# Moving twelve transposes of expert tiles between two stages, and a switch of row buffers by five rows

## The reference

```python
x += g1 * Mix(RMSNorm(x) * (1 + sc1) + sh1)    # three mixers, merged by gates, then ONE output projection
x += g2 * PEER(RMSNorm(x) * (1 + sc2) + sh2)

def run(xb):                                   # PEER, per block of tokens
    q = (xb @ w_q).reshape(blk, 8, 2, 128)
    s = einsum("thpd,pnd->thpn", q, keys)      # key scores, 2 x 128 sub-keys per head
    sv, si = top_k(s, 16)
    cand = sv[:, :, 0, :, None] + sv[:, :, 1, None, :]
    best, pos = top_k(cand.reshape(blk, 8, 256), 16)     # -> eidx, one of 16384 experts
    g = softmax(best)
    act = gelu(einsum("thkd,td->thk", u_tab[eidx], xb))
    return einsum("thk,thkd->td", g * act, v_tab[eidx])
```

## Time and profile before

| | us |
|---|---|
| median of 3 executions | 5041.49 |
| lowest, highest | 5041.38, 5047.62 |
| the profiled execution | 5041.38 |
| its span in the trace | 5039.7 |
| PE busy | 4756.8 (94%) |
| DVE busy | 2928.9 (58%) |
| POOL busy | 1867.7 (37%) |

### The profile page before, as it was taken

One profiled execution on the slowest core, in us unless ns is written; L12 is line 12 of the kernel. 1 busy time (PEld: TensorE's weight loads), 2 busy tenths in 40 slices (PEclk: granted clock), 3 DMA queues, 4 the chain that ended last, 5 costly groups with the idle time before them and its releaser, 6 DMA issues.

```text
span 5039.7 us, 84473 instructions
## 1 busy us (share of the span) xinstructions
PE 4756.8 (94%) x25204; PEld 3777.5 (75%) x25204; DVE 2928.9 (58%) x5739; ACT 1064.9 (21%) x2658; POOL 1867.7 (37%) x2649
## 2 busy tenths in 40 slices
PE   7999989889999999999989998898899999999998
PEld 5877777658777777777768877775678777777776
DVE  2653432424699788666636434324246997876665
ACT  1012111211111577000011121113111116760000
POOL 4541230125234444444445313301342344444543
PEclk9999999889999999999999999998899999999999
DMA  7774789688579999999977648995885899999998
GB/s 284 260 234 159 262 276 304 192 281 328 170 270 364 346 360 335 396 410 406 407 285 261 219 157 294 271 301 180 310 294 172 294 366 345 362 337 411 413 403 341
DMA packets 729817, 1519.25 MB, mean 301 GB/s; under 512 B 65296, under 2 KB 406288, under 8 KB 727392
## 3 DMA queue, kind: packets, MB, share of 16 engines
q0 software_dynamic: 256224, 888.06, 47.7%
q1 hardware_dynamic: 473216, 626.61, 36.4%
HBM read 1341.42 MB, written 307.21 MB: 327 GB/s over the span
## 4 chain that ended last, share of the span: by engine, by line
PE 78%; DMA 6%; issue 5%; DVE 5%; SPq 3%; DVEq 2%; ACT 1%; POOL 0%; POOLq 0%; another core or an unknown queue 0%; ACTq 0%
PE PS L1432 18%; PE PS L1375 17%; PE PS L760 8%; PE PS L872 8%; PE PS L1307 4%; PE PS L999 2%; PE PS L1326 2%; PE PS L1331 2%; PE PS L1387 2%; DMA u_rows<-arena 1%; SPq L526 1%; DMA xT<-u_rows,arena 1%; PE PS L783 1%; PE PS L795 1%; PE PS L1201 1%
## 5 line engine op out<-in xcount | busy, mean ns | idle before, releaser
L1375 PE MATMUL PS<-hT,ring 128*128 128x288 f32 x4096 | 1014.6, 406 | 0.0
L1432 PE MATMUL PS<-arena,ring 128*128 128x288 f32 x4096 | 993.9, 406 | 0.0
L1432 PEld LDWEIGHTS PS<-arena,ring 128*128 128x128 f32 x4096 | 778.1, 190 | 215.6 <-issue 1.0
L1375 PEld LDWEIGHTS PS<-hT,ring 128*128 128x128 f32 x4096 | 768.5, 190 | 201.6
L872 PE MATMUL PS<-hT,ring 128*128 128x272 f32 x2304 | 605.8, 409 | 4.6 <-DMA ring<-in_wst 4.6
L2065 DVE SCALAR_TENSOR_TENSOR PS<-xT,arena,PS 128x1024 f32<-128x1024 f32 x366 | 471.5, 1288 | 230.2 <-DMA xT<-v_rows,arena 214.9
L739 POOL DMA_INDIRECT xT<-u_rows,arena x410 | 400.6, 977 | 501.4 <-DVE arena L2056 407.3
L2292 ACT ACTIVATE arena<-PS 128x272 f32<-128x272 f32 (+20 forms) x578 | 220.8, 392 | 1500.3 <-PE PS L872 542.9
L2056 DVE CUSTOM_DVE_ANT_0 xT<-xT,PS 128x1024 f32<-128x1024 f32 x410 | 493.3, 1214 | 43.9 <-DMA xT<-u_rows,arena 39.8
L599 POOL DMA_DIRECT2D u_rows<-arena x864 | 478.0, 554 | 96.8 <-issue 23.9
L872 PEld LDWEIGHTS PS<-hT,ring 128*128 128x128 f32 x2304 | 439.5, 198 | 98.3 <-issue 15.0
(11 more groups left out here) (423 smaller groups left out, 5720.9 us busy)
## 6 DMA issues: line engine op xcount, KB each, us to landing
ring<-in_uv SPq DMA_DIRECT2D x512, 512.0 KB
ring<-in_wst SPq DMA_DIRECT2D x296, 512.0 KB
v_rows<-in_uv SPq DMA_DIRECT2D x256, 512.0 KB, 6.9
arena<-in_uv POOLq DMA_DIRECT2D x216, 512.0 KB, 6.6
u_rows<-arena POOLq DMA_DIRECT2D x864, 128.0 KB, 5.0
arena<-in_ck SPq DMA_DIRECT2D x96, 256.0 KB, 5.7
xT<-in_uv POOLq DMA_DIRECT2D x40, 512.0 KB, 6.2
u_rows<-xT POOLq DMA_DIRECT2D x160, 128.0 KB, 5.7
```

The lines of the kernel that those rows point to most:

```text
L1375: i = mm(PS[:, 2 + s % 2, 0:TD], ring[:, s, c, :], hD[:, c, :], start=(c == 0), stop=(c == DC - 1))
L1432: i = mm(PS[:, 2 + b, 0:TD], ring[:, s, j, :], WB[:, row, :], start=(row == 0), stop=(row == NK - 1))
```

## The change

Two constants and one loop. `U_OUT` goes from 12 to 24, and the loop behind an addition turns three tiles after each of the four steps of a round, where it turned two after each of the first three. The range of turns left for `head_best` follows from `U_OUT`: 6 tiles instead of 18 over eight heads. `N_SW` goes from 495 to 500 (512 rows, `(512 - 17) // 5 * 5` and `(512 - 12) // 5 * 5`).

```diff
--- before.py
+++ after.py
@@ -161,7 +161,7 @@
 C_TK = C_CD + 2048
 N_U1, N_UX, N_U2, N_U3 = 60, 20, 48, 0
 N_L = N_U1 + N_UX + N_U2
-U_MERGE, U_OUT = 18, 12
+U_MERGE, U_OUT = 18, 24
 U_FIRST, U_AT_OUT = 18, N_U1 + N_UX + U_MERGE + U_OUT
 U_OPEN = -(-N_U3 // RING) * RING + RING
 assert N_U1 % 6 == N_U2 % 3 == 0 and N_UX % 6 == 2 and N_L + N_U3 == NK and C_SC + 3 * DM <= C_IN2 and C_IN2 + 3 * DM <= C_SVI
@@ -185,7 +185,7 @@
 N_LEFT = N_OH - N_IN_U
 ROWS = row_order()
 NROW = len(ROWS)
-N_SW = (NROW - 17) // NBUF * NBUF
+N_SW = (NROW - 12) // NBUF * NBUF
 on_tensor = lambda n: ROWS[n][0] == "v" and ROWS[n][1] == 0 and ROWS[n][2] < N_LEFT
 T_ROWS = [n for n in range(NROW) if on_tensor(n)]
 V_ROWS = [n for n in range(NROW) if not on_tensor(n)]
@@ -2030,8 +2030,8 @@
                     residual(k * 4 + s, k * 4 + (16 + s), (0, HT), ps[:, 0, :])
                     residual(k * 4 + s, k * 4 + (16 + s), (HT, HT), ps[:, 1, :])
                     v.drain().then_inc(wo_v.sem, 1)
-                    for m in range(2 * s, min(2 * s + 2, 6)):
-                        turn_u(N_U1 + N_UX + U_MERGE + m, k * 2)
+                    for m in range(3 * s, 3 * s + 3):
+                        turn_u(N_U1 + N_UX + U_MERGE + m, k * 4)
             norm_query(l, 24, 32)
 
             order = {0: 0, 1: 1}
```

## The result

| | before | after |
|---|---|---|
| median, us | 5041.43 | 5099.04 |
| lowest, highest, us (4 executions each) | 5033.38, 5047.62 | 5088.18, 5124.47 |
| the profiled execution, us (its span) | 5041.38 (5039.7) | 5085.89 (5084.3) |
| granted clock, mean of the profiled execution | 0.971 | 0.967 |

The ratio after to before is 1.0125 (95% interval 1.0105 to 1.0143), which is 53 to 72 us more, 63 in the middle. The two medians of four executions lie 58 us apart; over all 26 executions of the changed kernel the median is 5103.7.

A forecast was written before the change was run, and what follows sets the result against it. PE was taken to bound the kernel, with the added projection turns limited by POOL's issuing and store landing. 5041.4 + 47 (turns, both layers) + 2 (later row switch) = 5090.4, said as 5090 us; range 5075 to 5106.

The forecast's parts named there:

- the root beneath the last turns: End of the projection: the norm's root, 7.9 us from the last addition, hides under some 10 us of turns; adds nothing.
- signs in numbers: Projection: additions some 10.4 us apart from the third on, reciprocal some 92 us after PE's first tile starts, instead of 69.
- Rival 1: Projection: turns fit DVE's idle time if a tile needs under 2.44 us; not slower, 5039 to 5043; 4 in 100.
- Part 1: Twelve turns per layer move from key-score stage to output projection: 23.5 us later per layer, 47 us in both.
- busy stretch: Elsewhere, 18 tiles turned in a row while PE streams weights: 3.52 us each; at that rate the projection's turns end 25.2 us later.
- the ring's loads: Projection: loads of PE's ring thin out when PE waits, so 23.5 us per layer was taken, below 25.2.
- The lower bound: Projection: POOL issues without pause, 3.29 us per tile, stores land 4.0 us after issue; reciprocal 19.2 us later per layer.
- Rival 2: Projection: stores land in 7 us instead of 4.0, 3.8 us per tile, 31.7 us late per layer, 5107; 12 in 100.
- The score stage: Key-score stage: removing 12 turns of 1.24 us DVE time gains 0, as PE bounds it; it keeps its 130 us.
- The lead before the first one-hots: End of score stage: first gathers start up to 3.7 us earlier, absorbed as DVE's 6.32 us wait becomes about 10.
- Cold tiles: Projection: PE's three late tiles at lower clock take 9.6 us, fit the 10.4 us step; price 0 to 2 us, none added.
- Part 2: Switch of row buffers at 500: later reload of x costs +2 us at layer 1's end, 0 at layer 0's.

The follow-up runs named there:

- both limits lifted: 24 turns as in the change, switch at 495, loads cut to 64 KB, two of four stores issued by ACT, against the kernel before: 5055.2 us, ratio 1.0029.
- The turns alone: Kernel before with 24 turns in the output projection, three after each addition, switch of row buffers left at 495: 5095.9 us, ratio 1.0120.
- experiment 6: Loads in the projection cut from 512 to 64 KB, against the kernel with 24 turns and the switch at 495: 5087.5 us, ratio 1.0100 to before.
- experiment 8: Kernel before with only the switch of row buffers moved from 495 to 500, 12 turns in the projection: 5048.2 us, ratio 1.0009.

## Why the prediction came out as it did

**The bound and its mechanism: right.** PE was the bound of the stage, DVE had room, and the turns were held up by the path of the tiles through POOL and its stores. The waits for the stores, the three late PE tiles, the gap before the query tiles, the root beneath the last turns and the untouched score stage are all in the trace as forecast. Less exact were the signs in numbers: the additions stand 9.8 to 13.2 us apart from the second on, 11.8 in the mean (10.4 forecast), and the reciprocal 96.5 us after PE's first tile (92). Rival 1 (it fits into DVE's idle time) would have needed under 2.44 us per tile; even with both limits lifted it was 2.64.

**Part 1: the step that was mis-sized.** I had two ends, POOL's pause-free 3.29 us per tile (19.2 us per layer) and the busy stretch's 3.52 (25.2 us per layer), and took 23.5 between them, on the ground that the ring's loads thin out when PE waits. The turns alone measured 25.5 and 25.6 us, 3.53 and 3.54 us per tile: the busy stretch, whole. In the changed kernel it was 27.7 and 26.5. So the term of 47 us stands against 51.1 (turns alone) and 54.2 (changed kernel). The reason for going below the nearer row was argued and not read, and experiment 6 shows that even with the DMA engines relieved POOL's pace is 3.45: the lower end, 3.29, was never to be had. I had read it off a single pair of sets. The next two sets of that same trace begin 3.34 and 3.89 us later (1217.43, 1220.77, 1224.66), which should have warned me. Some 0.3 us more come once per round of POOL's loop, and once early in the stage POOL pauses for some 2.7 us; what it does in either no view shows.

**What I called POOL's limit is two.** The lower bound took issuing as the one limit and added a fixed landing time of 4.0 us. It gave nearly the right rate, since the DMA engines bind at nearly the same pace (3.34 us per tile). Rival 2 named that second limit, the stores' landing, and had its size wrong: by the median they land no later than before, and its 7 us were too high. In the stage of layer 0 the DMA view gives the median from issue to landing last, first for after (1186 to 1290), then for before (1200 to 1280):

```profile
u_rows<-arena POOLq DMA_DIRECT2D x96, 128.0 KB, 4.7
```

```profile
u_rows<-arena POOLq DMA_DIRECT2D x49, 128.0 KB, 4.8
```

What changed is how often a turn has to wait for a landing. Rival 2's sum for the three buffers also left out the 0.75 to 0.8 us from a turn's end to POOL's next load.

For such a store the Trainium skill, "DMA: Bandwidth & Descriptors", section "Anatomy of one DMA", gives an estimate of 2.3 us by its formula. The traces do not agree: both kernels measure twice that. Nearest to it are the 2.7 us with small loads, at a DMA share of 0.74.

**The score stage: right.** Gain 0, by PE's 129.03 of 130 us. The lead before the first one-hots was larger than I said: the waits of 0.69 and 6.32 us became 8.26 and 6.66, together 7.9 us more where I counted 3.7, and the added wait stands one step ahead of the one-hots:

```profile
1671.60 0.72 DVE L2208 TENSOR_REDUCE rtmp<-RO 128x34 f32<-128x544 f32 x1 [8.26 <-ACT RO L2512]
...
1686.97 0.69 DVE L2225 TENSOR_TENSOR hT<-iota,RO 128x512 f32<-128x512 f32 x1 [6.66 <-ACTq L2524]
```

It was absorbed there all the same: from the first query tile to the first of these two it is 1671.60 - 1287.80 = 383.8 us, and as much before (1657.78 - 1273.96).

**Cold tiles: right, 0.** The late tiles took 10.2 and 10.7 us, where I had 9.6, and still fit, since the additions came 9.8 to 13.2 us apart and not 10.4. The fall of the clock shows in the row of the stage (0.89 against 0.97); no addition waits for PE behind it, so it has no price of its own.

**Part 2: right in size, +2 forecast, 1.2 to 2.6 measured**, by waits in two traces; whole executions can't tell it. In layer 0, where I took 0 within 0 to 2, the next layer's first matmuls come 1.5 us later against the last dense product in the changed kernel and 0.8 in experiment 8, about what two profiled executions differ by anyway.

**The sum.** 5041.4 + 54.2 + 2.6 = 5098. Of the 9 us by which I was short of the median of four, 7.2 are of part 1 and 0.6 of part 2. Against the median of all 26 I was short by 14, and some 6 us stand in no row that I read; that the four came out where the sum does is luck.

## What to carry to other kernels

Idle time of an engine in a stage is no room by itself: follow one item of the work that is to fill it (here load, turn, four stores, buffer free) through every engine and queue, and set the slowest rate against the stage's pace. If two candidates for that rate lie within some per cent, expect that removing one gains little, and test them together. Read a rate off a whole round of the loop and not off one pair. And where the trace has the same work under the same load, take its rate as it stands.

## What the runs showed that I had not expected

A fast DMA issuer is worth little while the DMA engines are full: at a share of 0.98 and 358 GB/s POOL idled 1 to 3 us per tile and a tile took 3.34 us. A DMA of 1 KB that nobody waits for cost POOL 0.73 us, and the stage 0.5 us per tile.

Executions of one kernel scatter widely, and those of the changed kernel no more widely than those of the one before: 26 executions of it ran from 5085.89 to 5124.47 us, and 53 of before, in three sets, from 5012.29 to 5055.04 (17 of them, the first set, within 19 us). In both the time goes with the mean granted clock: 0.962 to 0.968 in the changed kernel (correlation -0.75, about 4.9 us per 0.001), 0.968 to 0.975 in before (-0.82, about 5.2 us per 0.001). So the scatter goes with how long TensorE is granted less than its upper level of 2.4 GHz, which need not be its cause; where in the program it happens the executions without a trace don't tell, and I did not settle it.
